# A two-block model on one Trainium2 core: the key search done head by head, two neuron slabs held back instead of six, and part of a small GpSimd product moved to VectorE

## What is computed

```python
# first block: PEER, 8 heads, 128 keys a side, 16 best of each, 16384 experts
q = (xb @ wq).reshape(PEER_BLOCK, PEER_HEADS, 2, PEER_DKEY // 2)
s1 = jnp.einsum('thd,hnd->thn', q[:, :, 0], keys[:, 0]).astype(f32)
s2 = jnp.einsum('thd,hnd->thn', q[:, :, 1], keys[:, 1]).astype(f32)
v1, i1 = lax.top_k(s1, PEER_TOPK)
v2, i2 = lax.top_k(s2, PEER_TOPK)
cand = (v1[..., :, None] + v2[..., None, :]).reshape(PEER_BLOCK, PEER_HEADS, PEER_TOPK * PEER_TOPK)
sc, ci = lax.top_k(cand, PEER_TOPK)
e = (jnp.take_along_axis(i1, ci // PEER_TOPK, axis=-1) * PEER_NKEYS
     + jnp.take_along_axis(i2, ci % PEER_TOPK, axis=-1))
g = jax.nn.softmax(sc, axis=-1)
hid = jnp.einsum('thkd,td->thk', u[e], xb).astype(f32)
a = (jax.nn.gelu(hid, approximate=False) * g).astype(xb.dtype)
return jnp.einsum('thk,thkd->td', a, v[e])
# second block: gated delta rule over chunks of 64 tokens
a = jnp.where(strict, jnp.einsum('bhnid,bhnjd->bhnij', k_beta, k) * decay, 0.0)
sol = lax.linalg.triangular_solve(a + eye, rhs, left_side=True, lower=True, unit_diagonal=True)
```

## Time and profile before

| what | before |
|---|---|
| median of 3 runs | 3917.52 us (3915.14 to 3923.86) |
| the profiled execution, whole | 3911.82 us |
| its span in the trace | 3910.0 us |
| around the span | 1.82 us |
| PE, DVE, ACT, POOL busy | 93%, 64%, 39%, 19% |
| mean granted clock of PE | 0.967 |
| select, from the first query slab to the last one-hot | 560 to 1139.6 us |
| last matmul of the merged stream | 1074.4 us |
| first v slab | 1206.7 us |
| gated delta rule | 1855 to 2740 us |

### The profile page before, as it was taken

The page is one execution under the profiler, slowest core; times in us unless marked ns, Lnnn a source line. Parts: engine busy times, 40 slices in busy tenths (PEclk is TensorE's granted clock), DMA queues, the critical chain, the costliest instruction groups (busy, mean ns, idle before and its releaser), DMA issues. The chain is left out here.

```text
span 3910.0 us, 60019 instructions
## 1 busy us (share of the span) xinstructions
PE 3644.2 (93%) x24325; PEld 3397.9 (87%) x24325; DVE 2510.8 (64%) x5009; ACT 1519.7 (39%) x2704; POOL 762.4 (19%) x658
## 2 busy tenths in 40 slices
PE   7999999999979999999888899998899999979999
PEld 5777879999978999999788888887799999968999
DVE  5664346998978888989576666666543434565342
ACT  4555333335643333333434333332432334444241
POOL 0000004775423333332121221111000011010000
PEclk9999999999999999999899999998899999999999
DMA  3112224677879898988252332221132212112221
GB/s 120 60 65 72 91 90 135 235 233 234 272 240 342 319 346 322 338 323 317 54 79 47 59 60 54 59 51 41 50 99 91 92 44 66 62 53 81 95 95 60
DMA packets 208147, 542.29 MB, mean 139 GB/s; under 512 B 18664, under 2 KB 92904, under 8 KB 207872
## 3 DMA queue, kind: packets, MB, share of 16 engines
q1 hardware_dynamic: 99792, 341.22, 25.3%
q0 software_dynamic: 42048, 150.49, 13.8%
q10 hardware_dynamic: 66032, 46.75, 3.8%
HBM read 492.14 MB, written 46.25 MB: 138 GB/s over the span
## 5 line engine op out<-in xcount | busy, mean ns | idle before, releaser
L104 PE MATMUL bank<-Xh,wh 128*128 128x256 f32 (+3 forms) x3680 | 1225.6, 333 | 40.8 <-DVE Xl L131 21.0
L104 PE MATMUL bank<-Xl,wh 128*128 128x256 f32 (+3 forms) x3680 | 1161.1, 316 | 0.0
L104 PE MATMUL bank<-Xh,wl 128*128 128x256 f32 (+3 forms) x3680 | 1160.4, 315 | 0.0
L125 ACT ACTIVATE wh<-raw 128x1024 fp32r<-128x1024 f32 (+1 forms) x632 | 587.7, 953 | 681.4 <-PE bank L104 582.3
L131 DVE TENSOR_TENSOR wl<-raw,wh 128x1024 fp32r<-128x1024 f32 (+1 forms) x539 | 573.9, 1083 | 422.1 <-ACT wh L125 418.5
L104 PEld LDWEIGHTS bank<-Xh,wh 128*128 128x128 f32 x3680 | 710.6, 193 | 109.2 <-issue 63.1
L104 PEld LDWEIGHTS bank<-Xl,wh 128*128 128x128 f32 x3680 | 711.3, 193 | 17.9
L104 PEld LDWEIGHTS bank<-Xh,wl 128*128 128x128 f32 x3680 | 708.2, 192 | 20.8
L131 DVE TENSOR_TENSOR H<-H,bank 128x256 f32<-128x256 f32 (+3 forms) x394 | 182.8, 469 | 314.2 <-PE bank L104 312.1
L104 PE MATMUL bank<-aah,wh 128*128 128x384 f32 x1024 | 349.7, 341 | 13.9 <-DVE wl L131 12.3
L104 PE MATMUL bank<-aal,wh 128*128 128x384 f32 x1024 | 347.5, 339 | 0.0
(11 more groups left out here) (337 smaller groups left out, 6038.9 us busy)
## 6 DMA issues: line engine op xcount, KB each, us to landing
raw<-in_u SPq DMA_DIRECT2D x128, 512.0 KB, 3.8
raw<-in_v SPq DMA_DIRECT2D x128, 512.0 KB, 5.4
raw<-in_up SPq DMA_DIRECT2D x64, 512.0 KB, 3.4
raw<-in_down SPq DMA_DIRECT2D x64, 512.0 KB, 3.3
scratch<-gb ACTq DMA_DIRECT2D x12, 2048.0 KB, 11.1
gj<-scratch SPq DMA_DIRECT2D x32, 768.0 KB, 8.3
raw<-in_w_gdn SPq DMA_DIRECT2D x48, 512.0 KB, 3.4
raw<-in_w_att SPq DMA_DIRECT2D x36, 512.0 KB, 3.3
```

The costliest lines, as they stand in the source:

```text
L104: return Issued(self, self.q and self.q.matmul(out, l, r, start=start, stop=stop), 1)
L125: return Issued(self, self.q.activation(out, in_, func, **kw), 1)
```

## The change

It has three parts.

1. The searches of tiles 0 and 1 are taken out of `select()` and done head by head among the query slabs: `first_scores(h)` (PE, ACT) and `first_top(h)` (DVE, four lists) follow the copy of head h. The lists `vv` and `ii` are kept twice, `ca` uses the second half of `ss`. Tiles 2 and 3 are searched as before. `weights` is cut in two with a row's dot product between.
2. HELD goes from 6 to 2, so 94 slabs are merged, and the totals of `merge` are new: the stream now ends with the last one-hot group. Behind the merge the two held slabs have no side rows, each of the eight neuron slabs has two (before one or two in turn, and eight beside the held ones: 20 rows before, 16 now), and each of the twelve later pieces of two slabs has seven (before six and seven in turn).
3. In the gated delta rule POOL's two 128x384 products per (p, g) go. POOL's `unit_columns(p)` copies the identity's even columns into `tb`, nine chunks at once, ahead of time; DVE's `pair` computes the odd columns alone (two products of 128x192) and transposes right there; `level0` goes.

```diff
...
 AHEAD = 24
-HELD = 6
-ONEHOT = 3.1
+HELD = 2
+ONEHOT = 2.7
 NROW = 128
...
         do("keys")
-        WQ = {}
-        for hs in ((0, 1, 2), (3,), (4,), (5,), (6,), (7,)):
-            ss = [slab("w_q", h) for h in hs]
-            for h, s in zip(hs, ss):
-                WQ[h] = group(PD, by_slab(s), of_x(16, 528), 512, lambda k: xn2(16, k))
-            dense_together([WQ[h] for h in hs])
-            for h, s in zip(hs, ss):
-                done_with(s, WQ[h])
-                do("query", h)
-                given_back(WQ[h], "query", h)
...
+        VV = [alloc("vv", 2, 8, 16) for _ in range(2)]
+        II = [alloc("ii", 2, 8, 16) for _ in range(2)]
         CV = alloc("cv", 8, 16)
...
         assert top[0] <= S_AT
+        WQ = {}
+        def query_begin(h):
+            s = slab("w_q", h)
+            WQ[h] = group(PD, by_slab(s), of_x(16, 528), 512, lambda k: xn2(16, k))
+            return s
+        def query_end(h):
+            do("query", h)
+            given_back(WQ[h], "query", h)
+        def first_scores(h):
+            for s in range(2):
+                PA.take(("ks", "first", h, s))
+            do("first_scores", h)
+            for s in range(2):
+                PA.give(("ks", "first", h, s), ("ss", h, s))
+        ws = [query_begin(h) for h in range(3)]
+        dense_together([WQ[h] for h in range(3)])
+        done_with(ws[0], WQ[0])
+        for h in range(3):
+            query_end(h)
+        for h in (1, 2):
+            done_with(ws[h], WQ[h])
+        first_scores(0)
+        do("first_top", 0)
+        for h in range(3, 8):
+            s = query_begin(h)
+            for k, _ in enumerate(dense(WQ[h])):
+                if h == 3 and k in (2, 4):
+                    first_scores(k // 2)
+                    do("first_top", k // 2)
+            done_with(s, WQ[h])
+            query_end(h)
+            if h > 3:
+                first_scores(h - 1)
+                do("first_top", h - 1)
         top[0] = S_AT
...
                     if next(early, None):
-                        yield 1.25
+                        yield 2
...
             do("fixed")
-            for s in range(2):
-                scores_of(0, s)
-                yield 1
             for tl in range(4):
-                for s in range(2):
+                for s in range(2 if tl > 1 else 0):
                     do("top16", tl, s)
-                    yield 11.5
+                    yield 10
                     if tl < 3:
...
                     do("pick", tl, s)
-                    yield 7
-                    yield from some_early(tl, 2)
+                    yield 8
+                    yield from some_early(tl, 2 if tl > 1 else 3)
+                    if tl == 0:
+                        scores_of(2, s)
                 if tl == 0:
...
                 do("weights", tl)
+                yield from some_early(tl, 1)
+                do("weights_end", tl)
                 yield 3
...
-        merge((neurons_ahead(0, 4 * AHEAD - HELD), 9 * (4 * AHEAD - HELD)),
-              (select(), 4 * 60 + 1.25 * ROWS_EARLY + 5 + NT // 8 * ONEHOT))
+        ahead = neurons_ahead(0, 4 * AHEAD - HELD)
+        for _ in range(3):
+            next(ahead)
+        first_scores(7)
+        do("first_top", 7)
+        merge((ahead, 8 * (4 * AHEAD - HELD) - 3),
+              (select(), 40 + 80 + 64 + 14 + 2 * ROWS_EARLY + NT // 8 * ONEHOT))
...
             now(neurons_ahead(j, j + 1))
-            now(some(2 if j > 4 * AHEAD - HELD + 1 else 0))
-            if j == 4 * AHEAD - HELD + 2:
-                load(order[1])
+        load(order[1])
         for n in range(2):
...
                 neurons(order[n], (j,))
-                now(some(1 + j % 2))
+                now(some(2))
             load(order[n + 2])
...
                                                 (d, back(m, 1, 4)), (d, back(m + 1, 0, 0)))):
-                    side = some(6 + n % 2)
+                    side = some(7)
                     for j in (2 * (n % 2), 2 * (n % 2) + 1):
...
                         next(side, None)
-                    merge((steps, 16), (side, 4 + n % 2))
+                    merge((steps, 16), (side, 5))
                     if n % 2:
...
             do("keys_twice", p)
+            do("unit_columns", p)
             if p < 3:
...
                 PA.give(("ke", p, g), ("ke", p, g))
-                do("level0", p, g)
                 yield 1
...
+            def first_scores(h):
+                ps = [PS[clear(pe, PA, ("ks", "first", h, s))] for s in range(2)]
+                pe.wait_ge("query", h)
+                pe.wait_ge("keys", 0)
+                for n in range(4):
+                    tl, s = n // 2, n % 2
+                    i = pe.mm(ps[s][:, tl * 128:(tl + 1) * 128],
+                              QP[s * 64:s * 64 + 64, h, tl * 128:(tl + 1) * 128], KEY[s * 64:s * 64 + 64, h, :])
+                    if tl:
+                        i.then_inc("ks", "first", h, s)
+
             def key_scores(tl, s, hh):
...
+            def first_top(h):
+                dv.wait_ge("ss", h, 1)
+                jobs = [(n // 2, n % 2, SS[:, n // 2, n % 2 * 8 + h, :], S2[4 * (h % 2) + n][:, 0:128],
+                         VV[n // 2][:, n % 2, h, :], II[n // 2][:, n % 2, h, :].bitcast(U32)) for n in range(4)]
+                for tl, w, src, rest, v, i in jobs:
+                    dv.max8(v[:, 0:8], src).then_inc("top_a", tl, w, h)
+                for tl, w, src, rest, v, i in jobs:
+                    dv.wait_ge("top_a", tl, w, h)
...
+                    dv.max_index(i[:, 8:16], v[:, 8:16], rest).then_inc("top", tl, w, h)
...
                 dv.tt(four(DD.at[p], g), kq, four(DD.at[p], g), ALU.mult).then_inc("attn", p, g)
+                tb = three(TB.at[p], g)
+                odd = tb[:, :, 1:128:2]
+                clear(dv, TB, p)
+                dv.wait_ge("bb", p, g, 1)
+                dv.tt(odd, three(BB, g)[:, :, 1:128:2], b3(CS["lev0"])[:, :, 1:128:2], ALU.mult).then_inc("m", p, 0, g)
+                dv.wait_ge("m", p, 0, g)
+                dv.tt(odd, b3(IDENT)[:, :, 1:128:2], odd, ALU.subtract).then_inc("tb0", p, g)
                 dv.wait_ge("vtr", p, g)
...
                       BC[:, 3 * g:3 * g + 3, p:p + 1].to_broadcast([128, 3, 128]), ALU.mult).then_inc("bv", p, g)
+                dv.wait_ge("unit", p)
+                dv.wait_ge("tb0", p, g)
+                dv.squares(three(TA, g).rearrange("p c x -> p (c x)"),
+                           tb.rearrange("p c x -> p (c x)")).then_inc("ta0", p, g)
...
                     dv.squares(TA[:, 3 * g + n:3 * g + 3, :].rearrange("p c x -> p (c x)"), tb).then_inc("ta", p, lv, g)
-
-            def level0(p, g):
-                dv.wait_ge("tb0", p, g)
-                dv.squares(three(TA, g).rearrange("p c x -> p (c x)"),
-                           three(TB.at[p], g).rearrange("p c x -> p (c x)")).then_inc("ta0", p, g)
...
+            def first_scores(h):
+                for s in range(2):
+                    ac.wait_ge("ks", "first", h, s)
+                    ac.copy(SS[:, :, s * 8 + h, :],
+                            PS[PA.at["ks", "first", h, s]][:, 0:256].rearrange("p (t k) -> p t k", t=2)).then_inc("ss", h, s)
+
             def key_scores(tl, s, hh):
                 a0 = s * 8 + hh * 4
-                if tl:
-                    ac.wait_ge("top", tl - 1, s, 7)
+                ac.wait_ge("top", 0 if tl == 2 else 2, s, 7)
                 ac.wait_ge("ks", tl, s, hh)
-                ac.copy(SS[:, a0:a0 + 4, :], PS[PA.at["ks", tl, s, hh]].rearrange("p (a b) -> p a b", a=4)).then_inc(
+                ac.copy(SS[:, 0, a0:a0 + 4, :], PS[PA.at["ks", tl, s, hh]].rearrange("p (a b) -> p a b", a=4)).then_inc(
                     "ss", tl, s, hh)
...
-            def pair(p, g):
+            def unit_columns(p):
                 tb = clear(po, TB, p)
-                po.wait_ge("bb", p, g, 1)
-                po.tt(three(tb, g), three(BB, g), b3(CS["lev0"]), ALU.mult).then_inc("m", p, 0, g)
-                po.wait_ge("m", p, 0, g)
-                po.tt(three(tb, g), b3(IDENT), three(tb, g), ALU.subtract).then_inc("tb0", p, g)
+                po.tcopy(tb[:, :, 0:128:2], IDENT[:, 0:128:2].unsqueeze(1).to_broadcast([128, 9, 64])).then_inc("unit", p)
```

41 lines of the change are left out of this document (25 added, 16 removed).

## The result

The changed kernel takes 3893.09 us (median of 5 runs, 3889.55 to 3899.04), the kernel before 3917.43 in the same measurement: a ratio of 0.9938, 95% interval 0.9924 to 0.9953, so some 24 us faster. Forecast were 3846 us and a range of 3818 to 3878: right in sign, a third of the size. The profiled execution took 3897.2 us, with a span of 3895.4.

What follows compares the result with a forecast made beforehand. PE, busy 93% of the span, was taken as the bound, with time to win where it idles. Gains of 43 to the first v slab, minus 2, plus 27 make 68 us: 3844, median put at 3846, range 3818 to 3878.

Steps and rivals of the forecast that it cites:

- PE's unit costs: Slabs and one-hots on PE: 0.173 us a matmul, 4.15 a slab, 1.8 for a group's one-hot matmuls.
- The hole before the one-hots: PE's idle time before its first one-hot group: earlier DVE searches close it but for 2 us, 10 gained (0 to 12).
- The sum of 12: Cost of that hole: 7.08 us idle, 2.9 of the second period, some 2 of the slow first group.
- The spread: Slabs spread to the one-hots' end fill 36.4 us of PE idle time; last one-hot at 1110 instead of 1139.6.
- Behind the one-hots: From last one-hot to first v slab: 54 us (44 to 70), first v slab at 1164 instead of 1206.7.
- The later phases: Twelve pieces behind the first v slab have half a side row more each: 2 us lost (0 to 7).
- The delta rule: Gated delta rule: 44.2 us of PE's `ta` waits go, 17 us of DVE work comes; net 27 gained (0 to 50).
- the 17 us for 48 half products: DVE's added products in the delta rule, 353 ns for each 128x192 product, 17 us in all.
- a factor of 1.33 on the mean: Shared-interface contention in the delta rule: half products at 353 times 729/546, 471 ns, 23 us for 17, net 21.
- What came late next: Delta rule, once `ta` is early: `z`, `ke` and the first level's masks would be late next.
- The one on the delta rule: Rival: `ta` waits turn into waits for beta or the masks, nothing gained there, 3873 us; chance 0.14.
- a stretched one-hot group: Rival, slower than before: DVE's groups in the merge stretch; from 5.85 us all 68 are gone, 3929 at 6.2; chance 0.03.

Runs made afterwards that it cites:

- the run with POOL's splits: The changed kernel, but POOL instead of DVE takes the low halves of slabs 93 to 96: 3871.63 us, ratio 0.9878.
- six held: The changed kernel with HELD = 6 instead of 2 alone, DVE still splitting slabs 93 to 95: 3865.89 us, ratio 0.9857.
- the old number: The changed kernel with POOL taking four splits and 26 side rows a later phase instead of 28: 3868.25 us, ratio 0.9867.
- the old rows in both places: The changed kernel with POOL taking four splits, 20 side rows behind the merge and later phases as in the kernel before: 3868.00 us, ratio 0.9861.
- `qe` later: The changed kernel, but POOL's three qe products for a p each wait for DVE's first-level mask of the same group: 3877.92 us, ratio 0.9899.

## Why the prediction was wrong

By its own terms, against the profiled execution (3897.2 us against a sum of 3844: 53 us short). Of the 53, 25.7 are missing at the first v slab (1189.7 against 1164), 10.7 in the v stage (12.7 lost, 2 counted) and 16.7 behind it (10.3 gained in the traces, 27 counted).

- **PE's unit costs: right.** A period of 4.48 us against 4.41 to 4.48.
- **The hole before the one-hots: wrong, and made up elsewhere.** I had it closed but for 2 us, 10 gained, as "DVE should be there first". PE reached the one-hots at 893.0 and waited 3.41 us, and the second group started 7.85 us behind the first. The sum of 12 also counted the slow first group twice, since the 2.9 us of the second period hold it: the hole had cost 9.9 us, it costs 6.9 now, 3 gained. It never was DVE's search that made it: its weights were ready in both kernels when PE transposed them, without idling, at 908.08 before and 889.93 now. This transpose stands only one piece of a slab, 3.1 us, in front of the one-hots, and ACT's copy and DVE's first one-hots come behind it. From PE's transpose to its first one-hot matmul this took 10.2 us before and 6.5 now; putting the transpose further ahead wasn't tried. The first group came at 896.4, near my 893, because PE was at the hole 18.1 us earlier than before, where I had counted 13.5. So it is luck in part that 1110 came out to 0.2 us in the run with POOL's splits, which has the same hole (3.43 us).
- **The spread: the failing step.** I had seen four splits of DVE between the last groups and wrote that "four splits of about 1.1 us now stand between the last groups", as 4.4 us of work. Their price was a wait each: the split waits for ACT's `wh`, ACT stands behind copies of PE's one-hots, PE waits for the one-hots behind the split. 20.4 us of holes and half-clock matmuls behind them: the last one-hot comes 30 us later than in the run with POOL's splits, where the first had come 1.6 earlier. I had priced an instruction put in front of others by its duration alone and not asked what it waits for. With POOL as splitter, and with six held, the ring is gone, and 21.5 and 27.2 us come back.
- **Behind the one-hots: about right.** 49.8 us against 54; 53.3 with POOL's splits. The products with g stand 5.9 to 6.8 us apart, as the 6.33 that I took. Of the 9.0 us of waits that I read for the kernel before, 2 lie behind the first v slab. Two held slabs covered g's way as I had counted, but the six do so at no price.
- **The later phases: size wrong, the mechanism open.** I took 2 us of 0 to 7; it was 12.7 in this pair of profiles, 9 on the average of sixteen. I had priced the rows by their number alone; with the old number it stayed at 682.4, and only the old rows in both places gave 673.
- **The delta rule: the second failing step.** 27 us forecast, 14.2 measured. The mis-sized term is the 17 us for 48 half products: they took 38.5 (8.3 and 30.2). The mean of 353 ns came from rows whose second input lies in PSUM. The second half product reads two SBUF inputs and stands where POOL's three `qe` products run: up to 3.50 us, in six of eight p, in front of `ta`. Before, the block fell on two `z` behind `ta` (3.71 us together). The Trainium skill's rule (GPSIMD Engine Reference, section Key points) that the two contend for the shared interface agrees with this trace, 0.36 against 3.50 us. I had used it as a factor of 1.33 on the mean, 6 us in all; here it was a stop through all three of POOL's products. With `qe` later the half products took 19.5 us, and the stretch behind the v slabs came 30.6 us under the kernel before, near the 27. On the step of two, the first half product took 348 ns for 192 columns. The 353 of the earlier trace rows are no packed product either, since it leaves out blocks of columns; from the packed `xr<-bank,cst`, 553 ns for 384 columns and 419 for 256 in the same window, I estimate 352 for 192. No extra cost, then, which agrees with the Trainium skill, SBUF — State Buffer, note on SBUF "cachelines", that float32 may be strided up to four elements for free.
- **What came late next** was only in small part what I had named (`ke`, 7.1 us), and neither the masks nor beta. It was `vd`, 11.7 us, behind the long half product, and above all `vn` in ACT's queue, 17 us more of it.
- **The rivals.** The one on the delta rule was nearest in kind. The one on the other side, a stretched one-hot group, had the right place, but gave every group a little and not the last five a lot. (Its threshold should read 5.90 us a group, 4.48 and 1.42, and not 5.85.)

## What to carry to other kernels

When a stream of work is spread to the very end of another, look at the last rows of each engine's order: an instruction that waits there for an engine whose own next step depends on what stands behind it closes a ring, and costs a whole turn (here holes of 4.4 to 6.1 us on PE for 1.2 us of work). A constant that looks free, as the number of slabs held back, may be what kept such rows out. And when a product moves from GpSimd to VectorE, ask which GpSimd instructions will run at its new place: here, with both inputs in SBUF, its price was theirs.

## What was not expected of the hardware

- A VectorE product of 128x192 with both inputs in SBUF took 3.50 us instead of 0.36 while three GpSimd products ran back to back (2.96 us); with these later, one and then two together, its mean fell from 1257 to 464 ns.
- After holes of 4.4 to 6.1 us, a group of 16 one-hot matmul records took 3.45 to 3.76 us instead of 1.95. The granted clock over 1075 to 1140 was 0.85, and 0.50 from 1109 to 1113; with POOL's splits, without the holes, the groups there took 1.95 us throughout.
